# Layer norms of a transformer kernel: 1/rms applied when the products are evicted, input parts made bank by bank, squares folded into one ones-matmul, and a semaphore of their own for the per-layer vectors

## The chip, the cores and the metric

One core of one Trainium2 chip. The metric is the device time of one execution in microseconds, the median over runs. Engines: TensorE (PE, with its weight loads PEld), VectorE (DVE), ScalarE (ACT), GpSimd (POOL) and SyncE (SP, which here only issues DMAs).

## The reference, cut to what matters

The model has a first block (modulated half-FFNs around a gated linear attention and a Hyena mixer) whose result is normed with `final_norm_w`, and a second block of two layers on 256 tokens of width 1024. The change touches the norms around and in the second block:

```python
def rms_norm_2(x, gain, eps=NORM_EPS):
    y = xf * lax.rsqrt(jnp.mean(xf * xf, axis=-1, keepdims=True) + eps)
    return (y * gain.astype(jnp.float32)).astype(x.dtype)

# end of the first block
return rms_norm(h) * final_norm_w

# second block
for l in range(DEPTH_2):
    u = rms_norm_2(h, attn_norm[l])
    proj = jnp.einsum('bsd,dc->bsc', u, w_in[l])       # 7424 columns, split in 11
    ...                                                # three attentions, gates
    h = h + jnp.einsum('bsd,de->bse', merged, w_out[l])
    m = jnp.einsum('bsd,df->bsf', rms_norm_2(h, mlp_norm[l]), w_mlp_in[l])
    m = jnp.square(jax.nn.relu(m))
    h = h + jnp.einsum('bsf,fd->bsd', m, w_mlp_out[l])
return h
```

## The kernel before, in words

**Data.** The residual stream `h` lies in SBUF as 8 chunks of 128 features x 256 tokens, fp32. All weights come in one stream of 278 panels of 1 MB (128 x 2048 fp32). SP loads them into four slots of `landing` (L496), each as its slot comes free. A product in fp32 precision is made of three passes: weights and inputs are split in a high part (fp32r) and the rest, and `product` (L1578 to 1582) issues high x high, high x low, low x high. A column panel (256 output columns, all 1024 inputs) is 48 matmuls; a row panel (256 inputs, all 1024 outputs) is 48 too.

**Panels.** POOL makes the high weights (`high`, L520 and L521) into one of two buffers, as soon as PE has used the panel before last; then DVE makes the low weights (`low`, L594); then PE may start the panel. ACT and DVE make the high (L1231) and low (L602) parts of the inputs of row panels. DVE's, ACT's, POOL's and PE's streams are each written out by hand; all order between engines is by semaphores (`panel_used`, `hi_done`, `lo_done`, ...). `panel_loop` runs long stages of panels in a hardware loop. `layer_panel`, `at` and `following` turn the layer number into a panel number or a semaphore value.

**Start.** ACT's queue issues in this order: `mats`, `in_hyw`, `in_zT`, `in_window`, `in_hyc` (at 3.10 us), `in_xT`, `in_posemb`, `in_ctxT`, and last `v2all` (L1247, at 5.22 us), the gains and scalars of both layers. `mats` and `v2all` both count on `small_in`. PE multiplies the 36 modulation panels raw (L1747) with `c`, and after each but the first of a group of four runs `turn` (L1691 to 1698), a small matmul with a matrix of `mats`, which waits for `small_in` >= 32. Between them stand the steps of the Hyena filter (`filter_step`): the first (L1706) needs `in_hyw`, `in_zT`, `in_window` and `in_hyc`.

**A norm.** The row stage before it (down projection of the first block, `O_OUT`, or `O_MOUT`) accumulates in PSUM banks 4 to 7. In its last panel `by_banks` tells DVE after every two chunks (`sums_out`) that a bank is ready. DVE adds the bank to `h` (L963, L1149 or L1159); ACT squares the two chunks (`squares`, L1189); PE adds the squares over features with two ones-matmuls per bank (`norm_sum`, L1663), two of these groups inside the last row panel (`beside`), the others behind it. ACT makes 1/rms with Ln and Exp (L1184, L1185). Then, chunk by chunk, DVE scales h by gain and 1/rms (L627), ACT makes the high part (L1200) and DVE the low part (L635), and PE's first panel (`streamed`) takes each chunk as it is ready (`norm_lo`). At the end of the first block there are two in a row: `h` is scaled in place by 1/rms and `final_norm_w` (L977), and squared again for the first layer's norm.

**The layer loop.** DVE, ACT and PE each run both layers in one hardware loop (`Fori(0, LAYERS)`, L982, L1418, L1909). At its head DVE makes the low weights of the layer's first panel, ACT copies the layer's vectors from `v2all` to `v2` (L1422) and loads its table, and lambda of the differential attention is worked out (L988 to 994, L1911). Then come 30 projection panels: 5 of values (tokens on partitions), 25 of features, each evicted by ACT (`projected`, L1441, L1439, L1443) to SBUF; 18 panels have the head norms and rotations between them, 12 the attention scores (pairs n = 0 to 11; pairs 12 to 15 have no panel). In those pairs PE's turn of the weights (L1969) waits for DVE (L1043), and the retention scores (L1992) stand ahead of it. After the branches and `O_OUT` follows the MLP: 16 panels, ACT does ReLU (L1555) and the square (L1557), then 16 row panels. Every layer ends with squares and sums for a following norm, the last one too. SP writes `h` to `out` in one DMA of 1 MB (L506) after all four banks (`layer_done`).

## Time and profile before

| | us |
|---|---|
| median of 3 runs | 2130.72 |
| lowest, highest | 2118.73, 2134.42 |
| the profiled execution, device time | 2128.28 |
| its span, first to last instruction | 2126.5 |
| PE busy in it | 1979.3 (93%) |
| DVE, POOL, ACT busy | 1064.3, 600.6, 441.4 |

The profile is one execution. Each row of a timeline has the start in us, the duration in us, engine, line, operation, what is written from what, the size and count, and in brackets the engine's idle time before it with what released it. Instructions of one line that follow each other are merged; matmuls overlap, so a row's duration exceeds the time until the next.

### The profile page before, as it was taken

The numbers are of one execution on the slowest core, as the hardware profiler recorded it, in microseconds if no ns is written. First come the engines' busy times: TensorE is split into PE (matmuls) and PEld (weight loads), VectorE is DVE, ScalarE is ACT, GpSimd is POOL, SyncE is SP. The second block draws the span as 40 slices with busy tenths as digits, with TensorE's granted clock in tenths as the row PEclk, the third lists the DMA queues.
The fourth block names the chain that finished last, engine by engine and source line by source line (L and its number), as shares of the span: only waits on it lengthen the run. The fifth ranks groups of instructions, "written<-read, shape, count | busy, mean of one in ns | idle before, by whom it ended". The sixth has DMA issues, their size and how long they took to land.

```text
span 2126.5 us, 34194 instructions
## 1 busy us (share of the span) xinstructions
PE 1979.3 (93%) x13932; PEld 1791.5 (84%) x13932; DVE 1064.3 (50%) x1132; ACT 441.4 (21%) x797; POOL 600.6 (28%) x505
## 2 busy tenths in 40 slices
PE   4989999999998878899989999889999999888999
PEld 2448888887998867899989997779998999788999
DVE  1242222233447977644554675663455566574454
ACT  0220100101222221211121223422112212422211
POOL 0002222122134621234323332224332333123332
PEclk9899999999999989999999999999999999999999
DMA  8694222222233222355535343235553444234542
GB/s 316 226 345 191 94 99 99 99 99 79 80 119 129 100 79 85 119 180 185 189 119 178 134 145 119 100 121 183 189 179 140 159 142 156 80 120 154 182 179 99
DMA packets 43095, 307.97 MB, mean 145 GB/s; under 512 B 5024, under 2 KB 5408, under 8 KB 6048
## 3 DMA queue, kind: packets, MB, share of 16 engines
q1 hardware_dynamic: 40320, 292.66, 38.2%
q10 hardware_dynamic: 2656, 13.58, 1.7%
q8 instruction: 92, 1.51, 0.3%
q14 instruction: 27, 0.22, 0.0%
HBM read 303.08 MB, written 3.15 MB: 144 GB/s over the span
## 4 chain that ended last, share of the span: by engine, by line
PE 81%; DVE 9%; issue 5%; ACT 2%; POOL 2%; DMA 1%; ACTq 0%; DVEq 0%; POOLq 0%
PE ps L1580 23%; PE ps L1582 23%; PE ps L1581 23%; PE ps L1663 2%; PE ps L1747 2%; POOL whi L521 2%; DVE wlo L594 1%; DMA v2all<-in_vec 1%; PE ps L1735 1%; PE ps L1959 1%; PE ps L1698 1%; PE ps L1877 1%; PE ps L1983 1%; PE ps L1837 1%; PE ps L1942 1%
## 5 line engine op out<-in xcount | busy, mean ns | idle before, releaser
L1580 PE MATMUL ps<-xhi,whi 128*128 128x256 f32 (+1 forms) x3680 | 1117.6, 304 | 38.1 <-DVE xlo L602 21.2
L1581 PE MATMUL ps<-xlo,whi 128*128 128x256 f32 (+1 forms) x3680 | 1103.4, 300 | 0.0
L1582 PE MATMUL ps<-xhi,wlo 128*128 128x256 f32 (+1 forms) x3680 | 1102.8, 300 | 0.0
L594 DVE TENSOR_TENSOR wlo<-landing,whi 128x2048 fp32r<-128x2048 f32 x242 | 560.7, 2317 | 566.6 <-POOL whi L521 565.8
L1580 PEld LDWEIGHTS ps<-xhi,whi 128*128 128x128 f32 x3680 | 709.9, 193 | 71.9 <-DVE xlo L602 18.4
L1581 PEld LDWEIGHTS ps<-xlo,whi 128*128 128x128 f32 x3680 | 710.2, 193 | 22.5 <-issue 1.0
L1582 PEld LDWEIGHTS ps<-xhi,wlo 128*128 128x128 f32 x3680 | 709.8, 193 | 21.0
L520 POOL TENSOR_TENSOR whi<-landing,ones 128x128 fp32r<-128x128 f32 x242 | 127.0, 525 | 1499.0 <-PE ps L1582 1343.4
L521 POOL TENSOR_SCALAR whi<-landing 128x1920 fp32r<-128x1920 f32 x242 | 439.3, 1815 | 0.0
L1231 ACT ACTIVATE xhi<-big 128x512 fp32r (+3 forms) x66 | 45.8, 696 | 387.1 <-PE ps L1582 331.8
L759 DVE TENSOR_TENSOR big<-big,ps 128x512 f32 (+3 forms) x44 | 24.4, 555 | 200.2 <-ACT big L1219 200.2
L1580 PE MATMUL ps<-whi,xhi 128*128 128x256 f32 (+1 forms) x288 | 84.5, 293 | 8.8 <-DVE xlo L635 3.5
L1581 PE MATMUL ps<-wlo,xhi 128*128 128x256 f32 (+1 forms) x288 | 82.7, 287 | 0.0
L1582 PE MATMUL ps<-whi,xlo 128*128 128x256 f32 (+1 forms) x288 | 82.7, 287 | 0.0
L1443 ACT ACTIVATE big<-ps 128x512 f32<-128x512 f32 x50 | 29.9, 597 | 220.3 <-PE ps L1582 220.3
L1219 ACT ACTIVATE big<-ps 128x512 f32 (+3 forms) x44 | 21.6, 492 | 244.5 <-PE ps L1582 244.3
L602 DVE TENSOR_TENSOR xlo<-big,xhi 128x512 fp32r<-128x512 f32 (+1 forms) x82 | 62.0, 756 | 15.4 <-ACT xhi L1520 13.4
L1580 PEld LDWEIGHTS ps<-whi,xhi 128*128 128x128 f32 x288 | 56.8, 197 | 10.2 <-DVE xlo L635 3.6
L1663 PE MATMUL ps<-big,ones 128*128 128x256 f32 x176 | 45.8, 397 | 13.0 <-ACT big L1189 13.0
L1581 PEld LDWEIGHTS ps<-wlo,xhi 128*128 128x128 f32 x288 | 56.9, 198 | 0.0
L1582 PEld LDWEIGHTS ps<-whi,xlo 128*128 128x128 f32 x288 | 56.8, 197 | 0.0
L1747 PE MATMUL ps<-landing,cst 128*32 128x256 f32 x576 | 45.9, 447 | 11.2 <-DMA landing<-in_stream 11.2
(235 smaller groups left out, 1390.3 us busy)
## 6 DMA issues: line engine op xcount, KB each, us to landing
landing<-in_stream SPq DMA_DIRECT2D x278, 1024.0 KB, 4.8
spectra<-big ACTq DMA_DIRECT2D x2, 1024.0 KB, 10.0
ws<-spectra ACTq DMA_DIRECT2D x2, 1024.0 KB, 4.8
ws<-in_tabs ACTq DMA_DIRECT2D x1, 1280.0 KB, 5.5
ws<-in_hyc ACTq DMA_DIRECT2D x1, 1024.0 KB, 19.0
h<-in_xT ACTq DMA_DIRECT2D x1, 1024.0 KB, 23.5
ws<-in_ctxT ACTq DMA_DIRECT2D x1, 1024.0 KB, 27.6
ws<-in_lbrow ACTq DMA_DIRECT2D x1, 1024.0 KB, 14.6
```

Of the source, the lines that this page charges most:

```text
L520: pool.tensor_tensor(hi[:, 0:P], panel[:, 0:P], ones[:], ALU.mult)
L521: pool.tensor_scalar(hi[:, P:n], panel[:, P:n], 1.0, 0.0, ALU.mult, ALU.add).then_inc(hi_done, 1)
L594: v.tensor_tensor(wlo[:, s % 2], landing[:, s], whi[:, s % 2].bitcast(F32), ALU.subtract).then_inc(lo_done, 1)
L602: v.tensor_tensor(alo[:, r_phase % 2, :, 0:t], src, ahi[:, r_phase % 2, :, 0:t].bitcast(F32), ALU.subtract).then_inc(act_lo, 1)
L759: v.tensor_tensor(hid, hid, ps[:, bank, 0:t], ALU.mult).then_inc(hid_done, 1)
L1231: a.activation(ahi[:, j, :, 0:t], src(i + skip), ACT.Identity).then_inc(act_hi, 1)
L1443: ins = a.activation(chunks(PLAIN[i - N_VALUES], 2), two, ACT.Identity)
L1580: mm(out, w_hi, x_hi, start=first, stop=False, skip_group_check=True)
L1581: mm(out, w_hi, x_lo, start=False, stop=False, skip_group_check=True)
L1582: return mm(out, w_lo, x_hi, start=False, stop=last, skip_group_check=True)
L1663: last = mm(ps[:, bank, 0:T], ones[:], x, start=k == 0, stop=k == KD - 1, skip_group_check=True)
L1747: last = mm(ps[q:q + 32, j % 2, 0:COLS], cst[:, k], landing[:, j, k * COLS:(k + 1) * COLS], start=k < 4, stop=k >= 4, skip_group_check=True)
```

## The change

1. `v2all` counts on `v2all_in`; `turn` waits for `small_in` >= 16. The copy `v2` goes; `m2(l, name)` reads `v2all`.
2. The layer loops of DVE, ACT and PE are unrolled in Python (inner `panel_loop` loops stay), so waits take constants.
3. At four boundaries `h` isn't scaled by 1/rms before the product. As each bank is added, ACT makes the high part of h x gain and DVE the low part; the chunks are taken in the order 4 to 7, 0 to 3 by the row panel, the parts and the streamed panel. At the first boundary the gain is `final` x `attn_norm`, and the squares of h and of h x `final` are both made; `first_scales` and `first_rms` work out both 1/rms from them, and `h` itself is scaled by the final norm later (`finish_first`).
4. ACT squares each bank; DVE folds the four pairs of chunks to one 128 x 256 tile (`fold`); PE sums it with one ones-matmul (`boundary_sums`), after the second panel, outside the row panel.
5. 1/rms is applied at the evictions. Value panels: ACT, with a per-token scale that PE turns (`turn_rstd`). The 25 feature panels: DVE instead of ACT (`evict`). MLP: DVE does max(x, 0) x 1/rms (`relu`), ACT only the square.
6. The low weights of the panel behind a boundary are made before DVE's adds (`last=True` in `row_stage`), not behind the norm.
7. The sums behind the last layer go, and `out` is written in four DMAs, one per bank.

```diff
-            act.dma_start(v2all[:], ...).then_inc(small_in, 16)
+            act.dma_start(v2all[:], ...).then_inc(v2all_in, 16)
-                pe.wait_ge(small_in, 32)
+                pe.wait_ge(small_in, 16)
# DVE
+            def boundary(j, out0, end, add):
+                gain = boundary_gain(j)
+                def lows(b):
+                    for k in XHALVES[b]:
+                        dve.wait_ge(norm_hi, (5 + j) * KD + 2 * b + XHALVES[b].index(k) + 1)
+                        v.scalar_tensor_tensor(xlo[:, k, 0:T], h[:, k], gain(k), xhi[:, k, 0:T].bitcast(F32), ALU.mult,
+                                               ALU.subtract).then_inc(norm_lo, 1)
+                def step_of(b):
+                    add(b)
+                    if b:
+                        lows(b - 1)
+                residual(out0, end, step_of)
+                lows(3)
+            def fold(j, n=1):
+                dve.wait_ge(sq_done, 20 + 4 * j + 4)
+                for sq in squares_of[:n]:
+                    v.tensor_tensor(sq[:, 0], sq[:, 0], sq[:, 1], ALU.add)
+                    step(v.tensor_tensor(sq[:, 2], sq[:, 2], sq[:, 3], ALU.add))
+                    step(v.tensor_tensor(sq[:, 0], sq[:, 0], sq[:, 2], ALU.add))
+                    last = v.tensor_tensor(sq[:, 0, 0:T], sq[:, 0, 0:T], sq[:, 0, T:], ALU.add)
+                last.then_inc(folded, 1)
-            with dve.Fori(0, LAYERS) as l:
+            for l in range(LAYERS):
-                low(first[0], first[1] % SLOTS)
-                norm(0, h, lambda k: m2("attn_norm", k), None, 0, l)
+                def evict(i):
+                    dve.wait_ge(panel_used, l * PER_LAYER + (G_LAYER + i + 1))
+                    v.tensor_tensor(out2, ps[:, i % 2]..., rstd[:, 0]..to_broadcast([P, 2, T]), ALU.mult).then_inc(proj_out, 1)
                 for i in range(N_HEADS):
+                    if i > N_VALUES:
+                        if i == N_VALUES + 1:
+                            dve.wait_ge(inv_done, 2 * l + 1)
+                        evict(i - 1)
                     low_next(i)
+                    if i == 0:
+                        fold(2 * l, 2 if l == 0 else 1)
+                    if i == 1 and l == 0:
+                        first_scales()
+                    if i == 2:
+                        lam_parts()
+                    if i == 3 and l == 0:
+                        finish_first()
+                    if i == 4:
+                        lam_whole()
...
                     weights(n)
+                    if N_HEADS + n <= N_PROJ:
+                        evict(N_HEADS + n - 1)
                     if N_HEADS + n < N_PROJ:
                         low_next(N_HEADS + n)
...
+                boundary(2 * l + 1, at(sums_out, l, 3, base=12), end, lambda b: add_out(b).then_inc(res_done, 1))
+                low_min(1)
+                fold(2 * l + 1)
+                low_min(2)
+                dve.wait_ge(inv_done, 2 * l + 2)
+                relu(0, 0)
+                low_min(3)
+                relu(1, 1)
+                relu(2, 2)
+                low_min(4)
+                def relu_low(i, g, s):
+                    relu(i + 3, (s - first[1] + 3) % UNROLL)
+                    low(g + 5, (s + 5) % SLOTS)
# ACT, boundary(j)
+                for b in range(3):
+                    high(b)
+                    if j and b < 2:
+                        square(b)
+                if j == 0:
+                    square(0)
+                high(3)
+                for b in range(1 if j == 0 else 2, 4):
+                    square(b)
-                    if N_HEADS + n < N_PROJ:
-                        projected(N_HEADS + n)
# PE
+            def boundary_sums(j):
+                pe.wait_ge(folded, j + 1)
+                for n in range(2 if j == 0 else 1):
+                    last = mm(ps[:, 6 + n, 0:T], ones[:], squares_of[n][:, 0, 0:T], start=True, stop=True)
-                row_stage(..., by_banks=True, beside=lambda b: norm_sum(1, 0, b, ...))
-                for b in (2, 3):
-                    norm_sum(1, 0, b, ...)
+                row_stage(..., by_banks=True, order=K_ORDER)
                 for i in range(N_HEADS):
                     proj(i)
+                    if i == 1:
+                        boundary_sums(2 * l)
+                    if i == 2:
+                        turn_rstd()
+                    if i == 3:
+                        lam_sums()
# SP
-            sp.wait_ge(layer_done, 4 * (1 + LAYERS))
-            sp.dma_start(out, h[:]...).then_inc(out_done, 16)
+            for b, (k, _) in enumerate(XHALVES):
+                sp.wait_ge(layer_done, b + 1)
+                sp.dma_start(out[:, k * T:(k + 2) * T], h[:, k:k + 2]...).then_inc(out_done, 16)
```

## Rows read from the trace of the kernel before

**Rows 1.** Page, part 1: busy us, share of the span, instructions.

```profile
PE 1979.3 (93%) x13932; PEld 1791.5 (84%) x13932; DVE 1064.3 (50%) x1132; ACT 441.4 (21%) x797; POOL 600.6 (28%) x505
```

**Rows 2.** What PE waited for: us in total, times, longest.

```profile
PE ps L1698 <- DMA v2all<-in_vec: 17.4, 1, 17.4
...
PE ps L1747 <- DMA landing<-in_stream: 11.2, 2, 10.6
...
PE ps L1580 <- DVE xlo L635: 8.4, 4, 2.4
```

**Rows 3.** Timeline of PE, 30 to 50 us.

```profile
32.55 0.98 PE L1698 MATMUL ps<-mat,ws 128*128 128x2 f32 x4 [17.45 <-DMA v2all<-in_vec]
...
39.08 1.11 PE L1706 MATMUL ps<-ws 33*64 33x256 f32 x2
...
47.28 1.07 PE L1747 MATMUL ps<-landing,cst 128*32 128x256 f32 x16
```

**Rows 4.** DMA issues, 0 to 80 us: count, KB each, us to landing.

```profile
ws<-in_hyc ACTq DMA_DIRECT2D x1, 1024.0 KB, 19.0
```

**Rows 5.** Window table: us, busy of PE, PEld, DVE, ACT, POOL, PEclk, DMA share, GB/s.

```profile
20.00:30.00 10.00, 0.00 (x0) 0.00 (x0) 0.00 (x0) 0.00 (x0) 0.00 (x0) 1.00 1.01 419
```

**Rows 6.** Timeline at the end of the first block, PE and ACT.

```profile
1090.28 1.02 PE L1663 MATMUL ps<-big,ones 128*128 128x256 f32 x4
...
1111.44 0.39 PE L1580 MATMUL ps<-whi,xhi 128*128 128x256 f32 x1 [1.73 <-DVE wlo L594]
...
1118.98 0.60 ACT L1441 ACTIVATE ws<-ps 128x512 f32<-128x512 f32 x1 [8.63 <-PE ps L1582]
...
1124.74 0.60 ACT L1441 ACTIVATE ws<-ps 128x512 f32<-128x512 f32 x1 [5.16 <-PE ps L1582]
```

**Rows 7.** Timeline at the MLP norm of layer 0 and at the head of layer 1.

```profile
1413.42 1.13 PE L1663 MATMUL ps<-big,ones 128*128 128x256 f32 x4 [1.73 <-ACT big L1189]
...
1416.67 1.02 PE L1663 MATMUL ps<-big,ones 128*128 128x256 f32 x4
...
1429.02 0.39 PE L1580 MATMUL ps<-xhi,whi 128*128 128x256 f32 x1 [1.09 <-DVE wlo L594]
...
1609.39 1.02 PE L1663 MATMUL ps<-big,ones 128*128 128x256 f32 x4
...
1625.01 0.60 ACT L1441 ACTIVATE ws<-ps 128x512 f32<-128x512 f32 x1 [3.47 <-PE ps L1582]
```

**Rows 8.** Groups by form, second block: busy us, mean ns, idle before.

```profile
L627 DVE SCALAR_TENSOR_TENSOR big<-h,v,rstd 128x256 f32<-128x256 f32 x32 | 15.0, 478 | 8.2 <-ACT rstd L1185 8.2
...
L1159 DVE TENSOR_TENSOR h<-h,ps 128x512 f32<-128x512 f32 x8 | 5.5, 688 | 11.6 <-PE ps L1582 11.6
...
L1189 ACT ACTIVATE big<-h 128x512 f32<-128x512 f32 x24 | 15.0, 631 | 58.9 <-DVE h L1149 24.4 <-DVE h L1159 22.8 <-DVE h L963 10.2
...
L1200 ACT ACTIVATE xhi<-big 128x256 fp32r<-128x256 f32 x32 | 13.3, 418 | 10.4 <-DVE big L627 10.4
```

**Rows 9.** Timeline of POOL and DVE in the branches of layer 0.

```profile
1365.75 0.46 POOL L520 TENSOR_TENSOR whi<-landing,ones 128x128 fp32r<-128x128 f32 x1 [3.25 <-PE ps L1582]
1366.17 1.79 POOL L521 TENSOR_SCALAR whi<-landing 128x1920 fp32r<-128x1920 f32 x1
...
1363.94 2.47 DVE L1089 TENSOR_TENSOR big<-big,ps 128x512 f32<-128x512 f32 x4
1366.34 3.76 DVE L594 TENSOR_TENSOR wlo<-landing,whi 128x2048 fp32r<-128x2048 f32 x1
```

**Rows 10.** Timeline of DVE in the MLP of layer 0.

```profile
1466.21 2.30 DVE L594 TENSOR_TENSOR wlo<-landing,whi 128x2048 fp32r<-128x2048 f32 x1 [3.42 <-POOL whi L521]
```

**Rows 11.** Timeline of PE in the attention tail, pair 12.

```profile
1317.66 0.66 PE L1969 MATMUL ps<-mat,ws 128*128 128x128 f32 x4 [0.66 <-DVE ws L1043]
```

**Rows 12.** DMA issues, 2100 to 2127 us: count, KB, us to landing.

```profile
out<-h SPq DMA_DIRECT2D x1, 1024.0 KB, 3.9
```

**Rows 13.** Window table at the head of layer 1, columns as in rows 5.

```profile
1616.00:1624.00 8.00, 7.07 (x42) 7.07 (x43) 7.52 (x19) 3.48 (x10) 0.00 (x0) 0.65 0.38 133
```

More of the change, by code:

```diff
@@ L68 @@
 PANELS = G_LAYER + LAYERS * PER_LAYER
-DVE_LINKS, ACT_LINKS = 65, 8
+DVE_LINKS, ACT_LINKS = 65, 6
 R_DOWN1 = 0
@@ L1164, in _ @@
+                assert link[1] == per["dve_link"], link[1]
         @block.scalar
@@ L1202, in norm_parts, with norm_rms, boundary, high @@
-            def norm_parts(n, shift, dst0, l=None):
+            def norm_rms(n, bank):
+                act.wait_ge(sum_done, n + 1)
+                rms(rstd[:, n % 2], ps[:, bank, 0:T], D, 0, step).then_inc(rstd_done, 1)
+            def boundary(j):
+                gain = boundary_gain(j)
+                def high(b):
+                    act.wait_ge(res_done, 4 * j + b + 1)
+                    for k in XHALVES[b]:
+                        a.activation(xhi[:, k, 0:T], h[:, k], ACT.Identity, scale=gain(k)).then_inc(norm_hi, 1)
+                def square(b):
+                    k = XHALVES[b][0]
+                    last = a.activation(squares_of[0][:, b], h[:, k:k + 2].rearrange("p c t -> p (c t)"), ACT.Square)
+                    if j == 0:
+                        for c in range(2):
+                            last = a.activation(squares_of[1][:, b, c * T:(c + 1) * T], h[:, k + c], ACT.Square,
+                                                scale=m1("final", k + c))
+                    last.then_inc(sq_done, 1)
+                for b in range(3):
+                    high(b)
+                    if j and b < 2:
+                        square(b)
+                if j == 0:
+                    square(0)
+                high(3)
+                for b in range(1 if j == 0 else 2, 4):
+                    square(b)
@@ L1600, in token_panel, with row_panel @@
                 return last
-            def row_panel(s, r, outs, t, first, last, by_banks=False, beside=None):
-                for j, (out, opens) in enumerate(outs):
+            def row_panel(s, r, outs, t, first, last, by_banks=False, beside=None, order=range(KD)):
+                for n, j in enumerate(order):
+                    out, opens = outs[j]
                     for k in range(ROWK):
@@ L1643, in sums, with row_stage @@
                 return [(ps[:, j, 0:t], True) for j in range(KD)]
-            def row_stage(first, n, r0, r_phase, outs, t, by_banks=False, between=lambda: None, beside=None):
+            def row_stage(first, n, r0, r_phase, outs, t, by_banks=False, between=lambda: None, beside=None, order=range(KD)):
                 g0, phase = first if isinstance(first, tuple) else (first, first)
```

293 lines of the change are left out of this document (162 added, 131 removed).

## The prediction

> **What bounds the kernel now.** I read the page first: TensorE (PE) is busy 93% of a span of 2126.5 us [rows 1], so only gaps of PE and work taken off PE can pay. Then the table of what PE waits for: 17.4 us in one piece for the load of the per-layer vectors, and four stalls at the low input parts of a norm (DVE, L635) [rows 2]; these are what the change names. Then the timeline at both places. At the start PE stands until 32.55 us, because the first turn (L1698) waits for `small_in` >= 32, which counts the `v2all` load, last in ACT's queue [rows 3]. At a norm, PE ends the down or output products, adds four banks of squares with eight ones-matmuls (L1663), waits for Ln and Exp, then for a serial chain scale (DVE), high part (ACT), low part (DVE), and after its first streamed panel once more for the low weights of the second panel, since DVE was held by the norm [rows 6, 7]. A plain panel costs PE 5.76 us (ACT's evictions come 5.76 us apart [rows 6]), i.e. 0.12 us for each of 48 matmuls; I count each norm from the end of the last products to the start of the second panel behind it.
>
> **Start.** Afterwards the turn waits only for the matrices. Panels 2 and 3 then pass as they land, and PE's next stop is the filter matmul L1706, which needs the constants `in_hyc`, issued at 3.1 us and landing 19.0 us later, at about 22.1 us [rows 4]; before, it ran at 39.08 us [rows 3], 17 us later. That, and the whole wait of 17.4 us, is the upper end. But the queues moved 419 GB/s with a DMA share of 1.01 in 20 to 30 us [rows 5]: the transfers are full, and earlier requests only share. Up to 32 us the constants (some 5 MB) take about half; panels of 1.05 MB then come each 5 us, and each 2.5 us afterwards: panel 5 at 29.8, 6 at 33.7, 7 at 36.2 us. Before, panel 7 was worked on at 47.28 us [rows 3]. The gain is 11.1 us; bounds 5 us (if the wanted constants are pushed back by the extra panels) and 17.4 us. The low clock of the first stage could move it either way; I count no change.
>
> **The norm boundaries.** Four remain: first block to layer 0 (B0, which before was two norms, one behind the other), output to MLP in each layer (B1, B3), layer 0 to 1 (B2). Before: in B0 the last products end at 1090.27; two bank sums inside that panel hold the products up by 0.67 us each (four overlapping passes of 0.17 us, busy 1.02), so bare products would end at 1088.9. The second panel starts at 1111.44: 22.5 us [rows 6]. In B1 the products end at 1416.67; with the two sums and a stall of 1.7 us inside taken out, 1413.4; second panel 1429.02: 15.6 us. In B2 1609.39 becomes 1608.0, and the second panel starts at 1624.8 (its predecessor's eviction at 1625.01 less 0.2): 16.8 us [rows 7]. B3 repeats B1: 15.6 us.
>
> After, nothing waits for 1/rms. Per bank: add (0.69), two high parts on ACT (0.42 each), two low parts on DVE (0.48, pipelined to about 0.4 each) [rows 8]. But the low weights of the first panel now come before the adds, so the adds begin only about 1.1 us before the products end; call that moment 0. Adds of banks 0 and 1 end at 1.3, the first lows at 1.65, where PE starts. At 1.3 GpSimd begins the high weights of the second panel (0.46 and 1.79 us, 2.25 together). A DVE instruction with both inputs in SBUF that met them took 3.76 us, until GpSimd had ended and then its usual 2.3, while four that read PSUM passed beside them at 0.62 each [rows 9]. So the lows of bank 1 wait until about 3.9; then lows and adds alternate (1.4 us a bank): low parts done at 7.0, PE's streamed panel at 8.7. The low weights of the second panel end at 9.2, the second panel starts at 9.3, 8.2 us after the products' end. Then four additions fold the squares (0.69, 0.69, 0.69 and 0.4 us as the adds there, 2.4 together) [rows 8]; they, GpSimd's next high weights (2.25) and DVE's low weights (2.3) run one behind the other on the shared port, 7 us from 9.2: 16.2, where PE would want them at 15.4: 0.8 us lost. The one ones-matmul costs PE 0.34 us. B1 and B3 gain 15.6 - 8.2 - 1.1 = 6.3 us each. B2 also has the turn of 1/rms and the lambda sum, 0.7 us: 16.8 - 8.2 - 1.8 = 6.8. B0 has two scaled additions per bank (0.88 for the pair, of the form of L627 [rows 8]), and ACT three squares per bank (1.5 us); the lows end at 8.9, the second panel starts at 11.3 (10.2 after the products' end). Its squares end at 12.9, the double fold (4.9 us) starts behind GpSimd at 13.5, the next low weights come out at 20.8 instead of 17.1: 3.8 us lost; with 0.7 for sums and turn 4.5. Before, B0's second panel also ran slow, 7.4 us from 1111.44 to its eviction at 1118.98, 1.6 over 5.76 [rows 6]. I take this back: 22.5 - 10.2 - 4.5 + 1.6 = 9.4. Sum of the four: 9.4 + 6.3 + 6.8 + 6.3 = 28.8 us. Bounds: 16 us (each low blocked for a whole GpSimd instruction, 2 x 1.8 more per boundary, and the slow clock back in B0 and B2), 37 us (GpSimd gives way, no fold stall).
>
> The Trainium skill, "SBUF — State Buffer", on the shared port pair, states that a DVE operation with two SBUF inputs and a GpSimd operation exclude each other for whole instructions. By that rule the lows and folds are held, as above; without it the boundaries would give some 7 us more. The trace agrees: 3.76 against 2.3 us [rows 9].
>
> **Evictions moved to DVE.** 25 projection panels per layer and the ReLU of 16 MLP panels per layer go from ACT to DVE, 82 instructions of 0.69 us (as L1159, which reads PSUM too) [rows 8]. In the MLP DVE stands 3.42 us before each low part, waiting for GpSimd [rows 10], so an eviction fits in that wait, and it reads PSUM, so it isn't held by GpSimd [rows 9]. The same holds in the projections. If that cover failed, each would cost 0.7 less the panel's slack of about 1 us. So 0, bounds 0 and -16 us (0.2 us each). In the attention tail there is no cover: PE waits there for DVE's weights (0.66 us at the first pair [rows 11]), and the last eviction (panel 29) stands in that chain, also ahead of the retention scores: -0.65 us per layer, -1.3. The `v2` copies, one ACT table load of 1.28 us and the register arithmetic of the layer loop vanish; what stood on the path of that is in B2's count.
>
> **End.** Two bank sums inside the last panel go (1.35 us), and the 1 MB output (3.9 us from issue to landing [rows 12]) becomes four parts, of which only the last 0.25 MB is behind the end: at 0.41 MB per us 1.9 us less. 3.3 us.
>
> **Sum.** 11.1 + 28.8 + 0 - 1.3 + 3.3 = 41.9 us. The profiled execution took 2128.28 us (span 2126.5): 2086.4. The median of the runs shown is 2.4 us above it, so I predict 2089 us.
>
> **The rivals.** (a) The start gives nothing: the transfers are the bound there and PE only waits elsewhere. For it: 419 GB/s and a full DMA share [rows 5]; against it: PE waited for the stream twice only, 10.6 of 11.2 us at the very first panel [rows 2]. 2089 + 11 = 2100 us. (b) Clock: PE ran at 65% granted clock in 1616 to 1624, a mix of 1.2 and 2.4 GHz, behind a gap of some 7 us [rows 13]. If the shorter gaps keep 2.4 GHz everywhere, also in the stages behind the start, 10 to 15 us more go: about 2077. Against it: the stalls on the merge of the branches stay. (c) Evictions on DVE lengthen each panel by 0.2 us: POOL 2.25, eviction 0.69, low weights 2.3 and the waits between (some 0.4) sum to 5.6, close to 5.76. 2089 + 16 = 2105 us. (d) Slower than before: the same chain, if DVE's eviction and GpSimd's high part held each other in every panel. Each of the 82 panels would take 5.76 + 0.69: 82 x 0.69 = 57 us, less the 42 gained: 2146 us. It decides from 0.51 us per panel (42 / 82). Against it: DVE's instruction that read PSUM under GpSimd's wasn't held [rows 9]. (e) The change doesn't do what it says: PE gets its parts early but the boundary is held by the adds behind the low weights, with the folds never hidden: boundaries give 16: 2102 us.
>
> The Trainium skill, "TensorE: Matmul & The Clock Gate", on the two states of the clock, says PE is slow by default and sustained work releases it. The row at 65% agrees [rows 13]; by the rule fewer gaps mean more of 2.4 GHz, which is rival (b).
>
> **Chances.** Forecast (2080 to 2097) 0.52; (b) 0.16; (a) 0.12; (c) 0.09; (e) 0.07; (d) 0.04. The range from 2069 to 2108 us holds all but (d) and the far ends. A change under 1% (21 us) is about what a measurement of this kernel can't tell; faster by over 1% means under 2109.4: forecast, (a), (b), (e) and most of (c): 0.91. Within 1%: 0.05. Slower by over 1%: 0.04.
>
> **What would show it.** Right: the wait of L1698 for `v2all` gone and L1706 at about 22 us; the scaling of h by the final norm (L977) behind the first projections; streamed panels starting within 1 us of the last products in B1 to B3, about 3 us in B0; DVE lows of 0.4 us with one of them near 2 us under GpSimd; folds of 2.4 us; evictions of 0.69 us inside DVE's wait; panels still 5.76 us apart. Wrong: panels further apart than 5.76 us (then c or d), L1706 later than 30 us (a), a PE stall over 5 us in a boundary (e).

## The result, and the profile after

Four runs of the kernel after have a median of 2096.47 us (2092.37 to 2096.66), four of the kernel before 2132.57 us; the ratio is 0.9852, 95% interval 0.982 to 0.9884 (one run of before, of 2237.6 us, was in a slow state and is left out of the ratio; the other three have a median of 2130.72 us). Forecast: 2089 us, range 2080 to 2097: the measured median is inside it by 0.5 us. The profiled run took 2092.37 us with a span of 2090.3, 36.2 us less than the span of before; forecast 41.9.

The page, part 1, of after: the work of TensorE (PE) is 15.6 us less than in [rows 1], so more than half of what went had been waiting (busy time depends on the granted clock too, so the split is rough).

```profile
PE 1963.7 (94%) x13854; PEld 1776.9 (85%) x13854; DVE 1133.7 (54%) x1205; ACT 392.1 (19%) x724; POOL 601.3 (29%) x505
```

What PE waited for in after (us in total, times, longest), beside [rows 2]:

```profile
PE ps L1878 <- DMA landing<-in_stream: 17.5, 6, 11.2
...
PE ps L1704 <- DVE wlo L604: 9.1, 5, 4.9
PE ps L1704 <- DVE xlo L664: 7.5, 8, 1.0
PE ps L2111 <- DVE ws L1109: 5.7, 6, 1.4
PE ps L2134 <- DVE big L1044: 4.6, 2, 2.3
```

The wait for the per-layer vectors is gone and the landing of the stream (L1878) waits 6.3 us more; each boundary now has two waits of at most 1.0 us at the low input parts (L664); and a wait of the retention scores for an eviction (L2134) is new. The longest wait at low weights (4.9 us, at 153.33) is the start of the first block, which before had as well (5.0 us).

Where the time went is read best between marks that every kernel has, all in its own trace: the start of the last modulation matmul (S), the first matmul that sums `EMf` over its partitions in the first block (O, some 630 us behind S), the first rotation of layer 0 and of layer 1 (R0, R1), the first matmul of the retention's means in each layer (G0, G1), and the span's end. O to R0 holds boundary B0, G0 to R1 holds B1 and B2, G1 to the end holds B3 and the end. All in us; the experiments of the next section stand below the line of after.

| kernel | S | S to O | O to R0 | R0 to G0 | G0 to R1 | R1 to G1 | G1 to end | span |
|---|---|---|---|---|---|---|---|---|
| before | 153.0 | 628.2 | 379.2 | 178.6 | 333.2 | 178.6 | 275.7 | 2126.5 |
| after | 147.0 | 627.7 | 372.5 | 179.5 | 319.7 | 179.5 | 264.4 | 2090.3 |
| after_again | 151.2 | 628.7 | 372.8 | 179.5 | 319.6 | 179.6 | 264.4 | 2095.8 |
| e1_own_semaphore | 147.8 | 631.0 | 377.8 | 178.6 | 332.7 | 178.6 | 275.1 | 2121.6 |
| e2_unrolled_layers | 156.5 | 628.7 | 377.6 | 178.4 | 331.4 | 180.0 | 275.2 | 2127.8 |
| e3_shared_wait_back | 158.3 | 627.9 | 372.7 | 179.4 | 319.7 | 179.5 | 265.1 | 2102.6 |
| e4_evict_before_max | 148.2 | 629.1 | 372.8 | 178.5 | 320.2 | 178.5 | 265.9 | 2093.2 |
| e5_pe_sums_all | 147.9 | 627.8 | 372.7 | 179.5 | 325.6 | 179.5 | 268.6 | 2101.6 |
| e6_fold_one_later | 147.6 | 627.9 | 369.0 | 180.4 | 318.6 | 179.6 | 265.2 | 2088.3 |
| e7_inputs_later | 138.9 | 628.5 | 372.8 | 179.5 | 319.6 | 179.5 | 264.5 | 2083.3 |
| e8_less_gpsimd | 149.0 | 630.0 | 367.0 | 179.5 | 315.4 | 179.6 | 262.8 | 2083.3 |
| e9_three_together | 140.8 | 628.5 | 369.2 | 178.4 | 320.4 | 178.6 | 265.9 | 2081.8 |
| e10_gpsimd_held_back | 148.4 | 628.9 | 371.9 | 180.4 | 319.0 | 179.6 | 264.7 | 2092.9 |
| e12_adds_first | 147.7 | 628.0 | 367.8 | 179.9 | 321.7 | 179.8 | 266.7 | 2091.6 |

Before against after: start 6.0, B0 6.7, B1 with B2 13.5, B3 with the end 11.3, the attention 0.9 lost in each layer, and 0.5 in S to O.

What the table can tell is limited by the granted clock. Two traces of after agree within 0.3 us in each column behind O, but between different kernels a column that no edit reaches moved more: G1 to the end is 1.5 us longer in e4_evict_before_max than in after, and the windows 30 and 70 us behind G1 (us, PE busy, granted clock, DMA share, GB/s) show where, first of after, then of e4:

```profile
1855.90:1865.90 10.00, 8.10 (x57) 0.83 0.56 210
1895.90:1905.90 10.00, 8.12 (x64) 1.00 0.37 138
...
1857.30:1867.30 10.00, 8.09 (x51) 0.69 0.56 210
1897.30:1907.30 10.00, 8.13 (x55) 0.86 0.47 166
```

PE was busy as long, with fewer matmuls. S to O moved by up to 2.8 us (e1_own_semaphore), S itself by more.

The start in after, timeline of PE (start us, us, what; in brackets the idle time before it and what ended it), beside [rows 3]:

```profile
15.58 1.01 PE L1829 MATMUL ps<-mat,ws 128*128 128x2 f32 x4
...
22.46 1.93 PE L1878 MATMUL ps<-landing,cst 128*32 128x256 f32 x16 [2.10 <-DMA landing<-in_stream]
...
25.27 1.11 PE L1837 MATMUL ps<-ws 33*64 33x256 f32 x2
```

The turn (L1829) runs at 15.58 us where it stood until 32.55, and the filter matmul at 25.27 where it ran at 39.08. But PE now meets panels that haven't landed. The DMA issues say the same: the constants land no sooner than in [rows 4], and the vectors, whose wait is gone, 36.0 us behind their issue.

```profile
ws<-in_hyc ACTq DMA_DIRECT2D x1, 1024.0 KB, 19.4
...
v2all<-in_vec ACTq DMA_DIRECT2D x1, 39.0 KB, 36.0
```

B3 in after, timeline of DVE, POOL and PE (beside B1 in [rows 7]; the products end at 1898.9):

```profile
1899.19 2.69 DVE L664 SCALAR_TENSOR_TENSOR xlo<-h,v2all,xhi 128x256 fp32r<-128x256 f32 x2
1899.65 1.97 POOL L531 TENSOR_SCALAR whi<-landing 128x1920 fp32r<-128x1920 f32 x1
1900.11 0.36 PE L1704 MATMUL ps<-xhi,whi 128*128 128x256 f32 x1 [0.97 <-DVE xlo L664]
1901.94 0.38 PE L1704 MATMUL ps<-xhi,whi 128*128 128x256 f32 x1 [0.90 <-DVE xlo L664]
1902.41 0.87 DVE L664 SCALAR_TENSOR_TENSOR xlo<-h,v2all,xhi 128x256 fp32r<-128x256 f32 x2
...
1907.72 0.39 PE L1704 MATMUL ps<-xhi,whi 128*128 128x256 f32 x1 [0.22 <-DVE wlo L604]
```

PE starts 1 us behind the products; the pair of low parts that meets GpSimd's high weights takes 2.69 us, the next 0.87.

B0 in after, the same columns, beside [rows 6]; the products end at 1082.26:

```profile
1092.74 1.80 POOL L531 TENSOR_SCALAR whi<-landing 128x1920 fp32r<-128x1920 f32 x1
1093.03 2.05 DVE L678 TENSOR_TENSOR big<-big 128x512 f32<-128x512 f32 x1 [1.28 <-ACT big L1306]
...
1099.08 1.96 POOL L531 TENSOR_SCALAR whi<-landing 128x1920 fp32r<-128x1920 f32 x1
1099.31 3.87 DVE L604 TENSOR_TENSOR wlo<-landing,whi 128x2048 fp32r<-128x2048 f32 x1
...
1103.23 0.58 PE L1704 MATMUL ps<-whi,xhi 128*128 128x256 f32 x1 [2.66 <-DVE wlo L604]
```

The fold's first addition is held by one instruction of GpSimd (2.05 us, 0.68 without), and the low weights behind the fold meet the next one: 3.87 us, as in [rows 9]. PE stands 1.46 us before the sums and 2.66 us before the third panel, which then runs slow: 7.3 us to its end against 5.8, at a granted clock of 0.67 in 1103 to 1108 us.

### The profile page after: what moved, and what is told of

It is laid out like the page before. It is cut to its first block, busy times and chain, and to the rows that moved or that the text cites. A ratio compares the mean times of both kernels' runs of the same rounds, so it can differ in the third digit from the quotient of the medians.

```text
span 2090.3 us, 33307 instructions
## 1 busy us (share of the span) xinstructions
PE 1963.7 (94%) x13854; PEld 1776.9 (85%) x13854; DVE 1133.7 (54%) x1205; ACT 392.1 (19%) x724; POOL 601.3 (29%) x505
## 4 chain that ended last, share of the span: by engine, by line
PE 79%; DVE 11%; issue 4%; POOL 2%; ACT 2%; DMA 2%; SPq 0%; DVEq 0%; POOLq 0%; ACTq 0%
PE ps L1704 23%; PE ps L1706 22%; PE ps L1705 22%; DVE wlo L604 2%; POOL whi L531 2%; PE ps L1878 2%; DMA landing<-in_stream 2%; PE ps L1866 1%; PE ps L2101 1%; PE ps L2008 1%; PE ps L1829 1%; PE ps L2125 1%; DVE xlo L664 1%; PE ps L1794 1%; PE ps L1968 1%
## 5 line engine op out<-in xcount | busy, mean ns | idle before, releaser
L1367 ACT ACTIVATE xhi<-big 128x512 fp32r (+3 forms) x66 | 45.8, 696 | 386.0 <-PE ps L1706 332.8
L1878 PE MATMUL ps<-landing,cst 128*32 128x256 f32 x576 | 47.8, 461 | 17.7 <-DMA landing<-in_stream 17.5
L1878 PEld LDWEIGHTS ps<-landing,cst 128*32 128x32 f32 x576 | 17.1, 124 | 43.3 <-issue 29.4
L1096 DVE TENSOR_REDUCE smx<-ps 128x2 f32<-128x512 f32 x32 | 22.1, 690 | 52.3 <-PE ps L2101 52.3
## 6 DMA issues: line engine op xcount, KB each, us to landing
spectra<-big ACTq DMA_DIRECT2D x2, 1024.0 KB, 10.1
```

What stands on the lines that cost most here:

```text
L1096: lstep(v.tensor_reduce(st[:, 0:2], ps[:, 2 + 2 * (n % 2):4 + 2 * (n % 2), 0:T], AX, ALU.max, negate=True))
L1367: a.activation(ahi[:, j, :, 0:t], src(i + skip), ACT.Identity).then_inc(act_hi, 1)
L1878: last = mm(ps[q:q + 32, j % 2, 0:COLS], cst[:, k], landing[:, j, k * COLS:(k + 1) * COLS], start=k < 4, stop=k >= 4, skip_group_check=True)
```

## The experiments

Each kernel differs from before or after by what its diff shows; the profile of each is one run, the ratios are to runs of before in the same session.

**The start alone, added to before and taken from after.**

```diff
-act.dma_start(v2all[:], ...).then_inc(small_in, 16)
+act.dma_start(v2all[:], ...).then_inc(v2all_in, 16)
...
-pe.wait_ge(small_in, 32)
+pe.wait_ge(small_in, 16)
...
+act.wait_ge(v2all_in, 16)
 with act.Fori(0, LAYERS) as l:
```

> The kernel before with one edit: the load of the per-layer vectors counts on a semaphore of its own, ScalarE waits for it ahead of the layers, and TensorE's turn (L1698 there) waits for the matrices alone. Theory: this part alone brings what the start brought in the trace of after, where the pass over the modulation panels ended at 153.33 us in place of 159.46: 6.1 us, so about 2122 us for a profiled run that was 2128.28. Rival A (the forecast's own term): 11.1 us, about 2117. Rival B: the stall was hidden by the landing of the stream anyway, 0 to 2 us, 2126 to 2128. The trace should show no stall on the vectors' landing, more stalls on the landing panels, and the panels of the first 57 us at 1.9 us each.

Measured: 2121.08 us median, ratio 0.9963 (0.9946 to 0.9979), some 8 us. In the trace S came 5.2 us sooner; S to O is 2.8 us longer and O to R0 1.4 shorter, which the edit doesn't explain, and every stretch behind is that of before within 0.6 us.

```diff
 pe.wait_ge(small_in, 16)
+pe.wait_ge(v2all_in, 16)
```

> The kernel after with one edit: TensorE's turn waits for the per-layer vectors again. Theory: the start of before comes back, the pass over the modulation panels ends at 159.5 us in place of 153.3, and everything behind it is shifted by the same 6.1 us: 2098.5 us for a profiled run that was 2092.4. Rival: part of it is taken up later (DMA runs ahead behind the start), so under 3 us at the end; other rival: 11 us.

Measured: 2104.42 us median, 8 to 10 us over the two medians of after (2096.47, 2093.84). In its trace S comes 11.3 us later than in after, and all that follows is after's within 0.7 us. So by pairs of traces the edit of the start is worth 5 to 11 us, and what makes the spread is PE's clock. Windows of 10 us (us, PE busy, granted clock, DMA share, GB/s), first of e3_shared_wait_back:

```profile
40.00:50.00 10.00, 10.00 (x64) 0.50 0.82 285
50.00:60.00 10.00, 10.00 (x46) 0.50 0.62 249
60.00:70.00 10.00, 10.00 (x46) 0.50 0.68 231
70.00:80.00 10.00, 10.00 (x53) 0.83 0.49 190
```

and of before, which has the same wait:

```profile
40.00:50.00 10.00, 9.68 (x85) 1.00 0.82 308
50.00:60.00 10.00, 10.00 (x47) 0.57 0.78 313
60.00:70.00 10.00, 10.00 (x46) 0.58 0.57 212
```

Behind the same standstill of some 17 us one run had full clock (2.4 GHz) around 47 us, where sixteen rows took 1.07 us [rows 3], and fell then, the other was at 0.50 (1.2 GHz) until after 70 us: S at 153.0 and at 158.3. Both levels follow the same order of work; what chose between them these runs don't show. A third trace with this wait, e2_unrolled_layers below, had the same spell at 47 us and still S at 156.5: there the clock was low later, 0.69 in 80 to 90 us. All profiles together are steadier than any pair: the three with the old wait have S at 155.9 in the mean, the nine with the new wait and the same loads at 148.3 (147.0 to 151.2), 7.6 us apart, close to the 8 us of the medians.

**After once more.**

> The kernel after once more, unchanged, in the same session as the two beside it. Theory: the order of the work fixes everything but the granted clock of the first 70 us; the marks behind 160 us stand at the same distances as in the first trace of after within 0.5 us, and the end of the pass over the modulation panels moves by up to 3 us. Rival: the clock varies elsewhere too, and the marks behind 160 us move by over 2 us against each other.

Measured: 2093.84 us median (2092.41 to 2097.84). The marks behind S stand as in the first trace, within 1.0 us in the 628 us up to O and 0.3 us in each stretch behind it; S is 4.2 us later, with a granted clock of 0.71 in 70 to 80 us where it was 1.00. The theory holds behind O; at S it was up to 3 us that was expected, and S to O moved by 1.0 where 0.5 was. So a difference under 5 us at S says nothing in a single pair, and behind O one of 0.5 us or more counts only where the granted clock is the same.

**What the start was bound by.**

```diff
-act.dma_start(h..., xT)  ...  act.dma_start(v2all[:], ...)
 ...
-for i in range(3):
-    mod_group(i)
+mod_group(0)
+mod_group(1)
+act.dma_start(h..., xT)  ...  act.dma_start(v2all[:], ...)
+mod_group(2)
```

> The kernel after with one edit: ScalarE issues the loads of the tokens, the positions, the context and the per-layer vectors behind the eighth modulation panel instead of at the head of the kernel. Theory: the start is held by the share of the DMA engines that the stream gets (415 to 420 GB/s in all, full from 10 to 40 us, the stalls on the landing 17.5 us of which 6.3 behind the first panel): about 3 MB less in that stretch lets the panels 3 to 8 land earlier and takes 4 to 6 us off the end of the pass over the modulation panels (153.3 us in after). Rival: TensorE at half its granted clock (matmul groups of 1.93 us a panel beside 1.07 later) and the work between the panels bound the start; then under 2 us. Other rival: the late loads now keep the first tokens from VectorE or hold later panels up: 0 to 5 us slower.

Measured: 2090.04 us median, ratio 0.9826 (0.9779 to 0.9872); S 8.1 us before that of after, and as much at the span's end less 1.1. The stalls on the landing behind the fourth panel (0.92 and 1.86 us in after) are gone; the last one of e7_inputs_later is at the fourth:

```profile
21.89 1.94 PE L1879 MATMUL ps<-landing,cst 128*32 128x256 f32 x16 [2.09 <-DMA landing<-in_stream]
```

The four loads moved bring 2.2 MB, at 420 GB/s 5.3 us of the queues. So the transfers' share did bound the start of after. By medians the gain is 4 to 6 us (after: 2093.84 and 2096.47), as expected; the 8.1 us of the trace are more, but the profiled run (2085.30 us) is the fastest of the four, whose others took 2088.96 to 2094.19, and S alone differs by some us from run to run with the clock.

**The loops over the layers written out.**

```diff
-with pe.Fori(0, LAYERS) as l:      (so on DVE and ACT)
+for l in range(LAYERS):
```

> The kernel before with one edit: the three loops over the two layers (VectorE, ScalarE, TensorE) are written out, so that no engine turns a loop between layer 0 and layer 1, and the copy of the layer's vectors is kept. Theory: the loop turn stands at one boundary only and is worth 0 to 2 us there (ScalarE's issue gap of about 2 us at the head of layer 1 lies on the chain), so 2126 to 2128 us; the rest of what the boundaries gained comes from the gain at eviction and the parts by banks. Rival: writing the layers out is a large part of the boundaries' gain, 4 us or more (2124 or less). Other rival: the longer code costs fetches, 1 to 3 us slower.

Measured: ratio 0.9993 (0.9973 to 1.0013): no change. The one stretch that holds the turn of the loop, G0 to R1, is 1.8 us shorter, within the 0 to 2 us expected, but some 0.5 us of it is a granted clock of 0.83 for 0.66 some 30 us behind G0; in layer 1 a granted clock of 0.83 in 1832 to 1842 us took 1.4 us back.

**The attention tail.**

```diff
 for n in range(PAIRS):
+    if N_HEADS + n <= N_PROJ:
+        evict(N_HEADS + n - 1)
     if n + 1 < PAIRS:
         top(n + 1)
     weights(n)
-    if N_HEADS + n <= N_PROJ:
-        evict(N_HEADS + n - 1)
```

> The kernel after with one edit: in the loop over the score pairs VectorE evicts the panel of the pair before ahead of the maximum of the next pair, instead of behind the weights of this one. Theory: the retention scores' stall of 2.31 us on the last eviction (at 1304.9 and 1804.1 us) goes, and nothing takes its place but part of the wait for the weights: 1.0 to 1.2 us a layer, 2.0 to 2.4 us in all (2090.1 us for a profiled run that was 2092.4). Rival: the eviction now delays the maximum and with it ScalarE's exponentials in each of the 16 pairs, and the wait of the weights' transpose (5.7 us over both layers) grows by more than the stall gives back: 0 to 3 us slower.

Measured: 2093.59 us median, not to be told from after's 2093.84 and 2096.47. In the trace R0 to G0 and R1 to G1 are 1.0 us shorter each, equal to before's; the waits of PE, against 5.7 us (L2111) and 4.6 us (L2134) in after:

```profile
PE ps L2111 <- DVE ws L1109: 7.3, 8, 1.6
...
PE ps L2134 <- DVE ws L1122: 0.6, 2, 0.3
```

The mechanism is shown (e9_three_together has it again, 1.0 us a layer), and the 2 us are below what the medians tell; in this trace the clock behind G1 took 1.5 of them back, as shown above.

**Who adds up the squares.**

```diff
-pe.wait_ge(folded, j + 1)
+pe.wait_ge(sq_done, 20 + 4 * j + 4)
 for n in range(2 if j == 0 else 1):
-    last = mm(ps[:, 6 + n, 0:T], ones[:], squares_of[n][:, 0, 0:T], start=True, stop=True)
+    for x in range(8):
+        last = mm(ps[:, 6 + n, 0:T], ones[:], squares_of[n][:, x // 2, (x % 2) * T:(x % 2 + 1) * T],
+                  start=x == 0, stop=x == 7)
```

with the calls of `fold` left out.

> The kernel after with one edit: VectorE folds nothing; TensorE multiplies the eight parts of each set of squares with the ones itself (8 matmuls in place of 1 a set: 16 at the first boundary, 8 at the other three). A ones-matmul of 256 columns took 0.26 us of TensorE in the trace of before (45.8 us for 176). Theory: at the first boundary the stall goes (1.46 us before the sums, 2.66 us before the third panel) against 14 more matmuls, 3.6 us, and one low part that no fold delays: 0.5 to 3 us faster there; at the other three, where no stall stood behind the fold, each is 7 x 0.26 = 1.8 us slower. Together 2.5 to 5 us slower than after. Rival: VectorE's relief from the fold brings more than the matmuls cost everywhere (0 to 4 us faster).

Measured: 2104.25 us median, 8 to 10 us slower than after; by the table 0.2 us at B0, 5.9 at B1 with B2, 4.2 at B3. The direction was right, the size twice what was expected, and the reason is a misread row: one matmul of this fp32 kind leaves two records in the trace, so the 176 rows in 45.8 us were 88 matmuls. The eight matmuls of B3 stand as sixteen rows:

```profile
1921.84 3.61 PE L1754 MATMUL ps<-big,ones 128*128 128x256 f32 x16
```

The next product starts 3.27 us later: 0.41 us a matmul. Seven more cost 2.9 us at each of B1 to B3, 8.6 together (measured 10.1), and fourteen, 5.7 us, cancel the 5.3 us of B0's stall. So against eight matmuls the fold pays 10 us in this kernel, all of it at B1 to B3, where it is hidden.

**The fold in B0 one panel later.**

```diff
-if i == 0:
+if i == (1 if l == 0 else 0):
     fold(2 * l, 2 if l == 0 else 1)
-if i == 1 and l == 0:
+if i == 2 and l == 0:
     first_scales()
 ...
-if i == 1:
+if i == (2 if l == 0 else 1):
     boundary_sums(2 * l)
-if i == 2:
+if i == (3 if l == 0 else 2):
     turn_rstd()
```

> The kernel after with one edit, at the first boundary alone: VectorE makes the low part of the third panel ahead of the fold instead of behind it, TensorE takes the sums behind the third panel and the turn of 1/rms behind the fourth. Theory: the third panel starts at the second's end (1097.9 us in after, where it started at 1103.23), which gives 5.3 us, and the fifth panel, whose bank waits for the first value eviction, gives back about 1.4 us of it: 3.5 to 5.3 us faster than after between the end of the products and the first rotation. Rival: the low part, made while GpSimd makes the high part of the fourth, takes 3.9 us again and the chain of 1/rms is late for the fifth panel by as much as was gained: 0 to 1.5 us.

Measured: O to R0 3.5 us shorter, 2093.02 us median (ratio 0.9837, 0.9791 to 0.9883). The stalls of B0 that are left behind the streamed panel:

```profile
1106.55 0.38 PE L1704 MATMUL ps<-whi,xhi 128*128 128x256 f32 x1 [1.05 <-DVE wlo L604]
...
1114.32 0.30 PE L1704 MATMUL ps<-whi,xhi 128*128 128x128 f32 x1 [0.91 <-ACT ws L1567]
```

Instead of 4.1 us before sums and third panel, 1.05 us before the fourth and 0.91 for the first value eviction. In the attention of layer 0 0.9 us comes back; there the granted clock is 0.89 in 1294 to 1304 us, where after has 1.00 in 1297 to 1307.

**GpSimd beside DVE: taken away, and moved.**

```diff
+firsts = [l * PER_LAYER + G_LAYER + o for l in range(LAYERS) for o in (0, O_MIN)]
+left_out = {f + x for f in firsts for x in (1, 2, 3)}
 ...
+if isinstance(g, int) and g in left_out:
+    pool.tensor_scalar(hi[:, P:2 * P], panel[:, P:2 * P], ...).then_inc(hi_done, 1)
+    return
 pool.tensor_scalar(hi[:, P:n], panel[:, P:n], 1.0, 0.0, ALU.mult, ALU.add).then_inc(hi_done, 1)
```

> The kernel after with one edit that leaves part of the computation out: at each of the four boundaries GpSimd makes only the first 256 of 2048 columns of the high parts of the second, third and fourth panels (its main instruction of 1.8 to 2.25 us becomes one of about 0.15 us); nothing waits on other semaphores than before. Theory: VectorE's operations with two inputs from SBUF are held while GpSimd runs that instruction (a pair of low input parts 2.40 to 2.69 us beside 0.87 a pair later, the first add of the fold 2.05 beside 0.68, the low part of a panel 3.87 beside 2.29), and the price of it on TensorE is 1.0 us at each boundary (streamed start 0.9 us sooner) and 3 more at the first, where fold and low part stood in TensorE's way: 6 to 7 us faster than after in all. Rival: the low input parts are long because of what feeds them (the adds and ScalarE's high parts), and only the first boundary gains, 1 to 3 us.

This kernel leaves part of the high weights out, so its time only tells what GpSimd's instructions cost. Measured: 2084.52 us median, ratio 0.9791 (0.9745 to 0.9836); O to R0 5.5 us shorter, G0 to R1 4.3, G1 to the end 1.6: 11.4 us, more than the 6 to 7 expected: B0 gains 1.5 us more than expected, and B1 and B2 some 2 each and not 1. Part of that is clock: in B1 after has a granted clock of 0.73 in 1401 to 1406 us, behind its two stalls, and this kernel 1.00. The first pair of low parts in its B3, beside 2.69 us:

```profile
1893.74 1.19 DVE L677 SCALAR_TENSOR_TENSOR xlo<-h,v2all,xhi 128x256 fp32r<-128x256 f32 x2
...
1894.19 0.47 POOL L534 TENSOR_SCALAR whi<-landing 128x128 fp32r<-128x128 f32 x1
```

```diff
+held_back = {f + 1: (5 + j) * KD + 4 for j, f in enumerate(firsts)}
 ...
+if isinstance(g, int) and g in held_back:
+    pool.wait_ge(norm_lo, held_back[g])
```

> The kernel after with one edit: at each of the four boundaries GpSimd waits with the high part of the second panel until VectorE has made two pairs of the low input parts, so that it no longer runs beside the first pair. Theory: only the place of the hold counts, the first pair takes 0.87 to 1.0 us in place of 2.4 to 2.7 and the streamed panel's second wait (0.9 us at each boundary) goes; the hold comes back on the later pairs and on the low part of the second panel, which TensorE does not wait for at three of four boundaries: 2 to 3.6 us faster. Rival: VectorE is the bound of the whole boundary (adds, low parts, the low part of the second panel), and the same hold costs the same wherever it stands; then the second wait goes but the second panel starts as late as before or later: 0 to 3 us slower.

Measured: 2094.98 us median, ratio 0.9835 (0.9812 to 0.9858) beside 0.983 for after in the same session: nothing. (R0 to G0 is 0.9 us longer in its trace with a granted clock of 0.91 in 1299 to 1309 us, where after has 1.00.) B3 in its trace:

```profile
1901.84 0.89 DVE L675 SCALAR_TENSOR_TENSOR xlo<-h,v2all,xhi 128x256 fp32r<-128x256 f32 x2
1904.63 3.21 DVE L675 SCALAR_TENSOR_TENSOR xlo<-h,v2all,xhi 128x256 fp32r<-128x256 f32 x4
1904.71 2.07 POOL L535 TENSOR_SCALAR whi<-landing 128x1920 fp32r<-128x1920 f32 x1
1907.11 0.39 PE L1715 MATMUL ps<-xhi,whi 128*128 128x256 f32 x1 [0.81 <-DVE xlo L675]
1910.10 0.39 PE L1715 MATMUL ps<-xhi,whi 128*128 128x256 f32 x1 [0.58 <-DVE wlo L615]
```

The first pair is short, the next four low parts take 3.21 us in place of 1.66, and PE's three stalls (0.75, 0.81, 0.58) sum to 2.1 us as in after (0.97, 0.90, 0.22). The rival was right: DVE is the bound of the boundary, and the same hold costs the same wherever it stands within the boundary.

**The additions first.**

```diff
 def step_of(b):
     add(b)
-    if b:
-        lows(b - 1)
 residual(out0, end, step_of)
-lows(3)
+for b in range(4):
+    lows(b)
```

> The kernel after with one edit: at each of the four boundaries VectorE makes all four additions to h first and the four pairs of low input parts behind them, instead of a pair behind each addition; ScalarE's order stays. Theory (the interleaving is what lets TensorE start within 1 us of the products' end): the first pair is made behind two or three more additions (0.68 us each at three boundaries, 0.86 at the first), the streamed panel starts 1.3 to 2 us later, but VectorE's sum of work in front of the second panel is the same (2.7 us of additions, 4.3 to 5.1 of low input parts, 2.3 of the low weights), so the second panel starts nearly as late as before: 0 to 1 us slower at each boundary, 0 to 3 us in all. Rival: the later start passes through to the second panel, 1.3 to 2 us a boundary, 5 to 8 us in all slower.

Measured: 2093.47 us median, ratio 0.9841 (0.9802 to 0.988). B1 with B2 are 2.0 us slower, the upper end of the 1 us a boundary that was expected, and G1 to the end is 2.3 us slower, of which some 0.8 lies ahead of B3 (granted clock 0.66 in 1855 to 1865 us, where after has 0.83). But B0 is 4.7 us faster, which neither theory had. The streamed panel does start 2.72 us behind the products there, but the low parts no longer meet GpSimd (the eight in 3.39 us), ScalarE's squares are ready 2.2 us sooner (counted from the products' end), and the fold ends at 1098.5, ahead of GpSimd's next instruction:

```profile
1091.96 0.69 DVE L677 TENSOR_TENSOR big<-big 128x512 f32<-128x512 f32 x1 [0.84 <-ACT big L1305]
...
1098.50 2.28 DVE L604 TENSOR_TENSOR wlo<-landing,whi 128x2048 fp32r<-128x2048 f32 x1
...
1099.67 1.43 POOL L530 TENSOR_TENSOR whi<-landing,ones 128x128 fp32r<-128x128 f32 x1 [3.42 <-PE ps L1705]
...
1100.84 0.39 PE L1703 MATMUL ps<-whi,xhi 128*128 128x256 f32 x1 [0.46 <-DVE wlo L604]
```

Now GpSimd is the one that waits (1.43 us for an instruction of 0.46 [rows 9]). The low weights take 2.28 us in place of 3.87, the stall before the third panel is 0.46 in place of 2.66, and that panel takes 5.9 us in place of 7.3: the slow clock behind B0's stall went with the stall.

**Three gains together** (the diffs of e4, e6 and e7).

> The kernel after with the three edits that gained between two marks of their own traces: the evictions ahead of the maxima (2.0 us, from 1.0 in each layer between the first rotation and the retention's means), the fold one panel later at the first boundary (3.5 us) and the late loads of the inputs (8.1 us at the end of the pass over the modulation panels, of which 7.2 were left at 777 us). They stand in different stretches, so the theory adds them: 12.7 us less than the 2090.3 of after's span, 2077.6, and about 2083 to 2084 as the median. Rival: gains of single stretches are partly taken back by the granted clock and by the stream that lands later; 4 to 8 us.

Measured: 2085.59 us median (2081.46 to 2086.65), ratio to before 0.979 (0.9767 to 0.9814), where after in the same session had 0.983 (0.9807 to 0.9852): 8.2 us under after's 2093.84, the fastest kernel here that computes everything. By the table 6.2 of it at S, 3.3 in B0, 1.0 per layer in the attention, and 0.8, 0.7 and 1.5 us are given back in S to O, G0 to R1 and G1 to the end. So of the 12.7 us that were added up 8.5 came, a third less, and the traces say for most of it why. At S this kernel stands 1.9 us behind e7_inputs_later, and so it does from the second panel on (15.03 for 13.16, 72.97 for 71.06 us): its first panel landed 2.0 us later (12.50 for 10.48), and the rest of the start is the same. The 1.5 us at the end are the clock again: 0.69 in 1846 to 1856 us and 0.85 in 1886 to 1896.

## Why the prediction was right, point by point

The median lies in the range, near its upper end, and the mechanisms of the change came as forecast. But the total hides errors of both signs: the start, B0 and the tail gave 8.3 us less, the other boundaries with the end 2.1 us more.

- **Start, 11.1 us forecast, 6.0 in the profiled pair.** The step "panel 7 at 36.2 us" was nearly met: it was worked on at 38.87, and there 8.4 us had been gained. What failed is "the low clock of the first stage could move it either way; I count no change". From panel 7 on after gave back 2.4 us, since PE ran at its low level longer there: before had a spell at full clock around 47 us. Against a trace with the same wait and no such spell (e3) S is 11.3 us sooner, which is the forecast's number by chance of the clock; by medians, and by the mean of all profiles, the edit is worth about 8. So 11.1 was too high by 3 us even without the pair's own luck; the panels landed 2.7 us later than worked out at panel 7. Rival (a) is false (e1 gains 8 us alone). The filter matmul came 3 us later than the 22 forecast, behind the landing of panel 3.
- **B0, 9.4 forecast, 6.7 measured.** Second panel 9.85 us behind the products (10.2 forecast). The streamed panel started 1.0 us behind the products, where "about 3 us in B0" was given as a sign. The term that was mis-sized is "3.8 us lost" at the fold: PE came to the third panel 5.4 us late, 4.1 of it standing still, the rest the two sums between the two stalls. The working had DVE's low weights run behind GpSimd's high weights; in fact they met it again and took 3.87 us. And the 1.6 us that I "take back" for the slow clock did not come: the third panel took 7.3 us. e6 and e12 show both: without that stall 3.5 and 4.7 us go, the slow clock with it.
- **B1 and B2, 13.1 forecast, 13.5 measured; B3 and the end, 9.6 and 11.3.** Here the marks of the forecast stood: streamed start 1.0 us behind the products, one pair under GpSimd (2.69 us), second panel 8.8 us behind them in B3 (8.2 forecast), the fold off PE's path. Some 1.1 of the 11.3 us lie ahead of B3 and are no gain of the change: 30 us behind G1 before had a granted clock of 0.66 and after 0.83. What the late 1/rms and the earlier low weights (points 3 and 6 of the change) are worth each no run separates; e12 shows that taking the low parts bank by bank is worth 1 us or so at each of these three. e5 shows what the fold hides, 10 us. e8 confirms that the holds at the shared port are real (11.4 us go without GpSimd's work) and e10 that they can't be dodged by moving it, so rival (e) had the mechanism, with DVE as the bound of a boundary, but not the price.
- **Evictions on DVE, 0 forecast.** The MLP panels stay 5.76 us apart (1445.06 and 1450.82 below); DVE's instruction that reads PSUM takes 0.69 us and stands in the wait for GpSimd, which shrank from 3.42 [rows 10] to 1.54 us:

```profile
1445.06 0.69 DVE L1229 SCALAR_TENSOR_TENSOR ws<-ps,rstd 128x512 f32<-128x512 f32 x1 [1.17 <-PE ps L1706]
1447.29 2.29 DVE L604 TENSOR_TENSOR wlo<-landing,whi 128x2048 fp32r<-128x2048 f32 x1 [1.54 <-POOL whi L531]
1450.82 0.69 DVE L1229 SCALAR_TENSOR_TENSOR ws<-ps,rstd 128x512 f32<-128x512 f32 x1 [1.23 <-PE ps L1706]
```

  Rivals (c) and (d) are out.
- **Tail, -1.3 forecast, -1.8 measured.** The place was right (the last eviction ahead of the retention scores, L2134); e4 gives it all back.
- **Clock, rival (b).** Out as a whole: 2077 us needed full clock everywhere, and after still has 0.67 in B0, 0.73 in B1 and 0.83 behind G1.
- Sum: 41.9 against 36.2 us; 5.1 of the 5.7 us are the start, 2.7 B0, 0.5 the tail, less 2.1 at the other boundaries and the end and 0.5 in S to O. The forecast also put the median 2.4 us above the profiled run; it lies 4.1 above, 1.7 us more, and so 7.5 us above the 2089.

## What to carry to other kernels

Count a semaphore for what its waiter needs, and after that ask whose bytes fill the queues ahead of what is wanted first: removing the wait gave 8 us, moving 2.2 MB that were not needed yet gave 4 to 6 us more by medians. Where VectorE bounds a boundary, moving a hold within it changed nothing (e10); put what is not needed yet (the fold) behind what TensorE needs next. And read small gains between marks inside the trace, with the granted clock beside them: 1 us a layer was plain there, twice, that no median showed, and as much came and went with the clock alone in stretches that no edit touched.

## What the runs showed that was not expected

- With one and the same program two traces of after differ by 4.2 us at the end of the modulation pass and by at most 0.3 us in each stretch behind O. Of the 5.5 us between their spans 4.2 are made before S, all of it in the first 90 us, and 1.0 between S and O.
- In after the granted clock reads 1.00 from 10 to 60 us, while a panel's sixteen rows took 1.93 us, as at 0.50 in e3; from 63 us on they took 1.07. In this stretch the rows tell the level (1.2 or 2.4 GHz), the column doesn't.

```profile
50.00:60.00 10.00, 10.00 (x46) 1.00 0.74 273
60.00:70.00 10.00, 10.00 (x58) 1.00 0.45 165
```

- A ones-matmul on fp32 data leaves two records in the trace (eight matmuls, sixteen rows); counting rows as matmuls halved its price in one expectation.
- The hold at the shared port met every form here whose two inputs both lie in SBUF: TENSOR_TENSOR of 512 columns 2.05 for 0.68 us, of 2048 columns 3.87 for 2.29, SCALAR_TENSOR_TENSOR 2.69 for 0.87 a pair; while one that reads PSUM stayed at 0.68 to 0.69 us. It goes both ways: behind low weights that had begun, GpSimd's instruction of 128 columns took 1.43 us in e12's B0 instead of 0.46. The Trainium skill, "SBUF — State Buffer", on the shared port pair, has this exclusion as a rule, for the whole of the instruction that came first; the traces agree (3.87 us is about the rest of GpSimd's instruction and then the usual 2.29).
